# The opening of a one-core hybrid-layer kernel: reordering the transposes, the loads and the small projection that precede the steady weight stream

## The reference, cut to what matters

```python
h = rms_norm(x, lw['g_mix'])
proj = h @ lw['w_in']              # u (1024) | qkv (3072) | z (1024) | beta (8) | a (8) | two gates (2048 each)
y_s5 = s5_mixer(u, ...)            # 64 groups x 16 channels, complex diagonal state; uses s5_b, s5_c, lambda = exp(a dt)
y_dn = deltanet_mixer(qkv, z, beta, a, ...)
```

## The kernel before, in words

| slot | side jobs | units |
|---|---|---|
| 0 | const, par, x0, x1, s5a | - |
| 1 | x2, x3 | u0 |
| 2 | s5b, x4, x5 | u1 |
| 3 | s5par, h0, cst, x6, x7 | u2 |
| 4, 5, 6 | rows 0, 1, 2 | u3, u4, - |
| 7 | norm 0 | u5, u6 |
| 8, 9 | bmix 1, bmix 0 | u7 u8, u9 |
| 10 | bb 1, ct | u10, u11 |
| 11 | bb 0 | u12 |
| 12 | k0, ba | u13, u14 |
| 13 ... | s5 0 ... (three units each, then three or four) | u15 ... |

## Time and profile before

### The profile page before, as it was taken

How to read it: one execution, slowest core, us unless ns; L and a number is a source line. 1 busy time by engine, 2 the same in 40 slices (tenths; PEclk the granted TensorE clock), 3 DMA queues, 4 the chain that set the end, 5 groups by cost and what they waited for, 6 DMA issues and landing times.

```text
span 2157.6 us, 37104 instructions
## 1 busy us (share of the span) xinstructions
PE 2101.8 (97%) x14794; PEld 2050.4 (95%) x14794; DVE 1155.7 (54%) x1380; ACT 822.7 (38%) x1046; POOL 307.3 (14%) x375
## 2 busy tenths in 40 slices
PE   8989999999999999999999999999999999999997
PEld 7889999989999997999999999999999999999997
DVE  4598776945464438774444444343344444444553
ACT  6323333673232422534443333323333333333543
POOL 3634444000000104001110000000000000000111
PEclk8999999999999999999999999999999999999999
DMA  8433443543333556775444444444544444444442
GB/s 207 121 118 108 128 118 101 170 127 91 91 91 95 141 153 206 220 239 160 152 146 147 153 148 147 146 145 148 157 151 146 149 152 146 147 151 145 149 145 93
DMA packets 299266, 310.05 MB, mean 144 GB/s; under 512 B 24722, under 2 KB 290019, under 8 KB 298531
## 3 DMA queue, kind: packets, MB, share of 16 engines
q1 hardware_dynamic: 295476, 296.76, 45.0%
q0 software_dynamic: 3264, 11.64, 2.1%
q10 hardware_dynamic: 418, 0.12, 0.0%
HBM read 291.34 MB, written 17.14 MB: 143 GB/s over the span
## 4 chain that ended last, share of the span: by engine, by line
PE 88%; DVE 6%; ACT 2%; issue 2%; DMA 1%; SPq 0%; ACTq 0%; DVEq 0%
PE pg L1996 77%; PE side_a L2027 3%; DVE wlo L1329 2%; PE side_b L2027 2%; DVE cacc L1645 2%; PE side_b L2280 1%; PE side_a L2297 1%; DMA raw<-in_w_out 0%; PE side_a L1996 0%; ACT whi L897 0%; DMA par2n<-in_conv_w 0%; PE side_b L2108 0%; PE side_a L2298 0%; SPq L560 0%; PE side_a L2206 0%
## 5 line engine op out<-in xcount | busy, mean ns | idle before, releaser
L1329 DVE TENSOR_TENSOR wlo<-raw,whi 128x1024 fp32r<-128x1024 f32 (+1 forms) x528 | 647.1, 1231 | 737.7 <-ACT whi L897 736.1
L897 ACT ACTIVATE whi<-raw 128x1024 fp32r<-128x1024 f32 (+1 forms) x528 | 545.0, 1039 | 963.8 <-PE pg L1996 918.7
L1996 PE MATMUL pg<-xhi,whi 128*128 128x320 f32 x2816 | 885.0, 314 | 15.7 <-DVE wlo L1329 15.5
L1996 PE MATMUL pg<-xlo,whi 128*128 128x320 f32 x2816 | 873.8, 310 | 0.0
L1996 PE MATMUL pg<-xhi,wlo 128*128 128x320 f32 x2816 | 873.5, 310 | 0.0
L1996 PEld LDWEIGHTS pg<-xhi,whi 128*128 128x128 f32 x2816 | 532.2, 189 | 23.8 <-DVE wlo L1329 11.6
L1996 PEld LDWEIGHTS pg<-xlo,whi 128*128 128x128 f32 x2816 | 532.3, 189 | 0.8
L1996 PEld LDWEIGHTS pg<-xhi,wlo 128*128 128x128 f32 x2816 | 531.7, 189 | 0.0
L1996 PE MATMUL pg<-mhi,whi 128*128 128x320 f32 x704 | 217.7, 309 | 2.5 <-DVE wlo L1329 2.5
L1996 PE MATMUL pg<-mlo,whi 128*128 128x320 f32 x704 | 217.6, 309 | 0.0
L1996 PE MATMUL pg<-mhi,wlo 128*128 128x320 f32 x704 | 217.6, 309 | 0.0
(11 more groups left out here) (449 smaller groups left out, 2171.4 us busy)
## 6 DMA issues: line engine op xcount, KB each, us to landing
raw<-in_w_in SPq DMA_DIRECT2D x144, 512.0 KB, 3.7
raw<-in_w_gate SPq DMA_DIRECT2D x88, 512.0 KB, 3.6
raw<-in_w_up SPq DMA_DIRECT2D x88, 512.0 KB, 3.5
raw<-in_w_down SPq DMA_DIRECT2D x80, 512.0 KB, 3.6
raw<-in_w_out SPq DMA_DIRECT2D x32, 512.0 KB, 3.5
raw<-in_w_ple_gate SPq DMA_DIRECT2D x32, 512.0 KB, 3.5
raw<-in_w_a SPq DMA_DIRECT2D x16, 512.0 KB, 5.3
raw<-in_w_b SPq DMA_DIRECT2D x16, 512.0 KB, 4.5
```

The source lines that it names most:

```text
L897: act.activation(whi[:, r, 0:nk, :], raw[:, r, 0:nk, :], ACT.Copy).then_inc(w_hi, 1)
L1329: dve.tensor_tensor(wlo[:, r, 0:nk, :], raw[:, r, 0:nk, :], whi[:, r, 0:nk, :].bitcast(F32), ALU.subtract).then_inc(w_lo, 1)
L1996: ins = pe.matmul(out[:, m, 0:N], w, a, start=first and k == 0 and part == 0, stop=last and k == nk - 1 and part == 2)
```

## The change

- `side_fills` and `schedule`: x0 and x1 come ahead of par; a job `warm` holds the warm-up matmuls; `x+` is split off from x and holds ACT's `weighted` and DVE's `lows`; s5a and s5b come behind the x jobs of slots 1 and 2; s5par, h0 and cst behind x6, x7. The units of slots 10 to 14 are spread one by one.
- The store of `xt0` moves behind unit 9's load, and the four `cnat` loads move from SP's queue to POOL's, behind `tables()` and `h0_terms()`.
- `c_advanced` becomes two jobs, `cadv 0` with bb 0 and k0, and `cadv 1`; the padding becomes `pads`, the last job before s5.
- The small projection no longer uses high and low parts. DVE multiplies the 16 weight columns by the gain (`wbg`, padded to 32 columns) and PE multiplies it in plain float32 with `xt0`: 16 matmuls, feature tile k into PSUM rows 32 (k mod 4) to 32 (k mod 4) + 31. The four row groups are summed in the transposition, which multiplies by a 128 x 16 matrix `pick` of stacked identities.

```diff
-    keys = [("par",)] + [("x", j) for j in range(6)] + [("s5par",), ("h0",), ("cst",)] + [("x", j) for j in range(6, KD // 2)]
+    keys = [("x", 0), ("x", 1), ("par",)] + [("x", j) for j in range(2, KD // 2)] + [("s5par",), ("h0",), ("cst",)]
...
-    slot([("const",), ("par",), ("x", 0), ("x", 1), ("s5a",)], 0)
-    slot([("x", 2), ("x", 3)], 1)
-    slot([("s5b",), ("x", 4), ("x", 5)], 1)
-    slot([("s5par",), ("h0",), ("cst",), ("x", 6), ("x", 7)], 1)
+    slot([("const",), ("warm",), ("x", 0), ("x", 1), ("par",), ("x+", 0), ("x+", 1)], 0)
+    slot([("x", 2), ("x", 3), ("x+", 2), ("x+", 3), ("s5a",)], 1)
+    slot([("x", 4), ("x", 5), ("x+", 4), ("x+", 5), ("s5b",)], 1)
+    slot([("x", 6), ("x", 7), ("x+", 6), ("x+", 7), ("s5par",), ("h0",), ("cst",)], 1)
...
-    slot([("bb", 1), ("ct",)], 2)
-    slot([("bb", 0)], 1)
-    slot([("k0",), ("ba",)], 2)
+    slot([("bb", 1), ("ct",)], 1)
+    slot([("bb", 0), ("k0",), ("cadv", 0)], 1)
+    slot([("cadv", 1)], 1)
+    slot([("ba",)], 1)
+    slot([("pads",)], 1)
...
-                if n == 2 * RING - 1:
+                if n == 2 * RING + 1:
                     wait_drained(sp, ("x", KD // 2 - 1))
                     wait_drained(sp, ("x", KD // 2 - 2))
                     sp.dma_start(scr_x, xt0[:]).then_inc(sem("x_stored"), 16)
-                    sp.wait_ge(sem("row_squares"), 3)
-                    for r, c_ in enumerate((s5_c_re, s5_c_im)):
-                        src = c_[0].rearrange("(k g) c n -> (g c) k n", g=8)
-                        for h in range(2):
-                            sp.dma_start(cnat[:, r, :, h, :], src).then_inc(sem("cnat_landed"), 16)
...
                     elif what == "h0":
                         tables()
                         h0_terms()
+                        wait_filled(pool, ("x", KD // 2 - 2))
+                        wait_filled(pool, ("x", KD // 2 - 1))
+                        pool.wait_ge(sem("row_squares"), 3)
+                        for r, c_ in enumerate((s5_c_re, s5_c_im)):
+                            src = c_[0].rearrange("(k g) c n -> (g c) k n", g=8)
+                            for h in range(2):
+                                pool.dma_start(cnat[:, r, :, h, :], src).then_inc(sem("cnat_landed"), 16)
...
                     drain(copy(xt0[:, 2 * j:2 * j + 2, :], ps(key)[:, :, 0:N]), key)
-                    wait_drained(act, key)
-                    weighted(xt0, j, G_MIX)
+                elif what == "x+":
+                    wait_drained(act, ("x", a[0]))
+                    weighted(xt0, a[0], G_MIX)
...
                     root(a[0])
-                    act.wait_ge(sem("wba_landed"), 16)
-                    act.activation(wbhi[:], wba[:], ACT.Copy).then_inc(sem("wb_split"), 1)
...
                     b_discrete(a[0])
                     if a[0] == 0:
-                        dve.wait_ge(sem("wb_split"), 1)
-                        dve.tensor_tensor(wblo[:], wba[:], wbhi[:].bitcast(F32), ALU.subtract).then_inc(sem("wb_split"), 1)
+                        dve.wait_ge(sem("wba_landed"), 16)
+                        wait_drained(dve, ("par",))
+                        dve.wait_ge(sem("inv_ready"), 1)
+                        dve.memset(wbg[:, :, 2 * H:32], 0.0).then_inc(sem("wb_weighted"), 1)
+                        g = par1[:, G_MIX:G_MIX + KD].unsqueeze(2).broadcast_to([P, KD, 2 * H])
+                        dve.tensor_tensor(wbg[:, :, 0:2 * H], wba[:], g, ALU.mult).then_inc(sem("wb_weighted"), 1)
+                        dve.wait_ge(sem("ident_ready"), 1)
+                        dve.tensor_reduce(pick[:], ident[:].rearrange("p (q c) -> p c q", q=4)[:, 0:2 * H, :], AX.X, ALU.add).then_inc(sem("wb_weighted"), 1)
...
-                    drain(dve.tensor_copy(bafm[:], ps(key)[0:2 * H, 0, 0:N]), key)
+                    drain(dve.tensor_copy(bafm[:], ps(key)[:, 0, 0:N]), key)
...
+                elif what == "pads":
                     dve.wait_ge(sem("x_stored"), 16)
...
-                    c_advanced()
+                elif what == "cadv":
+                    c_advanced(a[0])
...
-                    pe.wait_ge(sem("wb_split"), 2)
-                    pe.wait_ge(sem("xlo_ready"), KD)
+                    pe.wait_ge(sem("wb_weighted"), 3)
+                    for j in range(KD // 2 - 2, KD // 2):
+                        wait_drained(pe, ("x", j))
                     out = begin(key)
                     for k in range(KD):
-                        for part, (w, x) in enumerate(((wbhi, xhi), (wbhi, xlo), (wblo, xhi))):
-                            ins = pe.matmul(out[0:2 * H, 0, 0:N], w[:, k, :], x[:, k, :], start=k == 0 and part == 0,
-                                            stop=k == KD - 1 and part == 2)
+                        q = k % 4
+                        ins = pe.matmul(out[32 * q:32 * q + 32, 0, 0:N], wbg[:, k, :], xt0[:, k, :], start=k < 4, stop=k >= KD - 4)
...
-                        ins = pe.transpose(out[0:n, 0, 16 * c:16 * c + 16], bafm[:, c0:c0 + n], ident[0:2 * H, 0:2 * H])
+                        ins = pe.matmul(out[0:n, 0, 16 * c:16 * c + 16], bafm[:, c0:c0 + n], pick[:], start=True, stop=True)
```

More of the change, by code:

```diff
@@ L343, in hybrid_layer @@
         wba = zpre.take("wba", [P, KD, 2 * H])
-        wbhi = zpre.take("wbhi", [P, KD, 2 * H], F32R)
         zpre2 = Zone(nc, arena_at, 8192 + 16384)
@@ L360, in hybrid_layer @@
         zba = Zone(nc, arena_at - 3 * N * 4, 3 * N * 4)
-        wblo = zba.take("wblo", [P, KD, 2 * H], F32R)
-        bafm = zba.take("bafm", [2 * H, N])
+        wbg = zba.take("wbg", [P, KD, 32])
+        bafm = zba.take("bafm", [P, N])
+        pick = zba.take("pick", [P, 2 * H])
         zd = Zone(nc, arena_at, arena)
@@ L1489, in b_discrete, with c_advanced, v @@
                     spread(bnat, 0)
-            def c_advanced():
+            def c_advanced(k):
                 wait_filled(dve, ("k0",))
[L1494 to L1508, removed]
+                tiles = slice(NT // 2 * k, NT // 2 * k + NT // 2)
+                def v(t, r):
+                    return t[:, r].rearrange("p k (q c) -> p (k q) c", q=4)[:, tiles]
+                lr, li = (sp5[:, e, tiles].unsqueeze(2).broadcast_to([P, NT // 2, 32]) for e in (3, 4))
+                tmp = ctmp[:].rearrange("p (t c) -> p t c", c=32)
+                o.step(dve.tensor_tensor(v(ctl, 0), v(ct, 0), lr, ALU.mult))
+                o.link(dve.tensor_tensor(tmp, v(ct, 1), li, ALU.mult))
+                o.step(dve.tensor_tensor(v(ctl, 0), v(ctl, 0), tmp, ALU.add))
+                o.settle()
+                o.step(dve.tensor_tensor(v(ctl, 1), v(ct, 1), lr, ALU.mult))
+                o.link(dve.tensor_tensor(tmp, v(ct, 0), li, ALU.mult))
+                dve.tensor_tensor(v(ctl, 1), v(ctl, 1), tmp, ALU.subtract).then_inc(sem("ctl_ready"), 1)
+                dve.wait_ge(sem("ctl_ready"), k + 1)
             def s5_tiles(hq):
@@ L1570, in side @@
                 what, a = key[0], key[1:]
-                if what == "x":
+                if what == "x+":
                     lows(xt0, a[0], a[0], G_MIX)
@@ L2031, in side @@
                 what, a = key[0], key[1:]
-                if what == "par":
+                if what == "warm":
                     pe.wait_ge(sem("ident_ready"), 1)
-                    out = begin(key)
+                    out = begin(("x", 0))
                     for k in range(16):
                         pe.matmul(out[:, 0, 0:P], ident[:], ident[:], start=True, stop=True)
+                elif what == "par":
                     pe.wait_ge(sem("par_landed"), 16 * 8)
+                    out = begin(key)
                     pe.transpose(out[:, 0, 0:81], par1n[:], ident[0:81, 0:81])
```

## The result

| us | before | after |
|---|---|---|
| median (6 runs each) | 2167.4 (2160.67 to 2168.64) | 2176.78 (2173.72 to 2177.89) |
| the profiled execution | 2159.32 | 2177.65 |
| its span | 2157.6 | 2175.9 |
| mean granted TensorE clock | 0.988 | 0.981 |
| first readout of s5 on PE (the **mark**) | 131.53 | 144.16 |

The ratio is 1.0048, with a 95% interval of 1.0033 to 1.0063: the change costs 9.4 us. The mark is where the opening ends and the steady stream of weights begins; most of what follows is read from it.

A forecast was written before the change was run, and what follows sets the result against it. PE, busy 97% of the span, was taken to bound the kernel. +16.0 us at u10, -5.65 and -2.1 summed to +8.2, which on the median gave 2175 us; range 2163 to 2185.

The forecast's parts named there:

- Steps 1, 2: Opening: transposes ahead of parameters gain 0.3 us at u0; later S5 scalars lose 2.4 at u2, 2.8 at u3.
- Step 3: SP's queue, free of `cnat`, loads u8 and u9 earlier: 2.4 us gained at the end of u9.
- Step 4: At `ct`, `cnat` loads behind POOL's tables make PE wait 18 us: 16 us lost at u10.
- The term for POOL's slow-down: POOL's tables and h0 terms run slower beside DVE's added splits: 1.0 us added, bounds 0 and 2.8.
- Step 5: Small projection in column groups takes 3.1 us instead of 7.12: 4 us gained.
- Step 6: `c_advanced` halved, units spread: u15's gap goes, 3.8 us of new gaps; 5.65 gained from u10 to u15, then 2.1.
- POOL doesn't gate `ct`: At `ct`, `cnat` lands before PE needs it; u10 waits only for its split: -9.7 us, 2157; chance 0.1.
- the loads drain slowly: `cnat` loads land one by one through POOL's queue; `ct` opens at 102.5: +9.5 on the forecast, 2184; chance 0.25.
- the change only shifts waits: `ct`'s wait is paid for by projection and halves: -2 to +5 us, `ct` opening at 86 to 90; chance 0.15.

The follow-up runs named there:

- e11: The kernel before with one number changed: store and `cnat` loads, still on SP's queue, two units later, behind unit 9; 2160.65 us, ratio 0.9973.
- e1: The changed kernel with the four `cnat` loads back on SP's queue, behind the store and unit 9's load; 2160.45 us, ratio 0.9974.
- e3: The changed kernel with the `cnat` loads on POOL's queue between tables and h0 terms; 2169.73 us in one run.
- e8: The kernel before with only the `cnat` loads moved behind POOL's h0 terms and the store behind unit 9; 2175.34 us, ratio 1.0053.
- e9: The kernel before with only the new order of the opening, S5 scalars later included; 2166.41 us, ratio 0.9996.
- e6: The kernel before with only the small projection changed (`wbg`, `pick`, 16 matmuls); 2159.11 us, ratio 0.9978.
- e7: The kernel before with only `c_advanced` in halves, `pads` and the units of the slots spread; 2162.91 us, ratio 0.9995.
- e10: The changed kernel with `cnat` loads on SP's queue, S5 scalars in their old places and units spread once more; 2152.50 us, ratio 0.9934.
- e2: The changed kernel with the `cnat` loads still on POOL's queue, but ahead of tables and h0 terms; 2160.44 us, ratio 0.9977.

## Why the prediction was right

The forecast was +8.2 us, 2175.0; it is +9.4, 2176.78, inside the range and in the class with the highest chance, by the mechanism foreseen. That 8.2 and 9.4 lie so near is in part luck: at the mark, where the steps can be checked, the two profiles are 12.6 us apart. Against that the steps stand like this:

| step | predicted | measured |
|---|---|---|
| 1, u0 | 20.7 | 20.74 |
| 2, wait before s5par | 3.3 | 3.18 |
| 2, u2 begins | 41.1 | 42.67 |
| 3, gap before u9; u9 | 0.6; 69.7 | 0.32; 70.59 |
| 4, tables start and end | 39.3, 84.1 | 39.49, 85.46 |
| 4, `cnat` lands; gap before `ct` | 93; 18 | 93.25; 17.16 |
| 4, u10 begins | 95.9 (+16.0) | 96.96 (+17.0) |
| 5, projection | 3.1 | 2.36 |
| 6, gaps before u12, u14 | 1.9, 1.9 | 3.10, 1.73 |
| 6, u10 to u15 | 31.8 (-5.65) | 35.1 (-2.3) |
| 6, two units from u15 | 7.1 (-2.1) | 7.1 (-2.1) |

**Steps 1, 2.** Right. u2 is 1.6 late of which 1.1 is the conv transposes: 2.75 at the lower clock, not the 1.65 of the row I used.

**Step 3.** Right in the sum (70.59 against 69.7), too small as a price. I gave SP's free queue 2.4 us; alone, without the later scalars in its way, it takes the whole gap of 3.4, and e11's interval on the whole is 2.2 to 9.8 us. The prediction had the S5 scalars eat this gain.

**Step 4.** Right in the mechanism and nearly in the size, shown from both ends (e1 to e3 take it out, e8 puts it in alone). The term for POOL's slow-down was too small: I added 1.0 us to 43.8, and the stretch took 46.0 here, 46.8 in e8 and 47.7 in e11, so 2.2 to 3.9 more. Over all profiles it took 41.8 to 48.9 us, and e9, where SP's queue is as before, has 47.0, so which part of the change slows POOL is not shown. The Trainium skill, SBUF — State Buffer, section "Who interferes with whom", has a DVE instruction with two SBUF inputs contend with a GpSimd instruction that reads SBUF; the rule goes both ways there, whichever issued first holding the other up, where the prediction named DVE alone. The 2.8 us that I worked out by that rule was nearer than my 1.0. The landing made up for it: 4.64 us behind the last issue, where I took 6 from loads of another size. `ct` took 3.7 at the lower clock, not 2.9, and u10 gave that back (3.7 for 5.3), so bb 0 began at 100.70 for 101.2.

**Step 5.** Right, 0.7 us too dear; e6 shows the gain alone.

**Step 6.** The step that failed in size: 5.65 us, of which 2.3 came. That figure held step 5's 4 us, so what it gave the halves and the spread was 1.65; measured, they cost some 2 us (2.3 less the projection's 4.3, from its first matmul to the unit behind it), though u10 was 1.6 shorter than the sum had it. Two terms did that. First, `cadv 0` took 5.4 us (104.26 to 109.65) and not 4.1: POOL's `phases(0)` ran beside it, and its operations took 0.69 to 1.12 us each where those of `cadv 1`, with POOL idle, took 0.69 throughout. Second, I let the lower clock end with u15's gap, but both new gaps brought it back, for 3.4 us each, of which PE loses half, 3.4 in all: u12 and u14 took 5.2 us each for the 3.5 that I had put down. e7 shows the outcome: alone, this part gains nothing that its interval (0.9982 to 1.0009) shows.

The **rivals**: that POOL doesn't gate `ct` falls with a gap of 17.16 that ends on the DMA. That the loads drain slowly, for 102.5, falls with the landing at 93.25. That the change only shifts waits would need `ct` open by 90.

What stays open is why the marks are 12.6 apart and the medians 9.4. The ratio's interval (7.2 to 13.7 us) holds both, the profile before is 8 us below its median and the one after 0.9 above, and marks of single executions carry the clock's stretches, 2.0 us of them in the case of e11. So the 1.2 us between forecast and median are no measure of the steps: against the marks the forecast is 4.4 short, 1.0 of it at u10 and 3.4 in step 6.

## What to carry to other kernels

A load belongs on a queue whose *preceding* work ends before the load is needed: count from the end of what is queued ahead of it, not from the queue's speed. On the fully busy engine two small gaps need not be cheaper than one larger, since each can bring the lower clock with it (both did in e7, one of e10's two did). And before four loads are moved to another engine's queue, try moving them two places down their own: here that is one changed number and worth 0.27% (0.10 to 0.45), as much as e1 with all the rest of the change.

## What the runs showed of the hardware

- The same four loads of 256 KB in 256-byte pieces take POOL 0.90 to 1.09 us each to issue, wherever they stand (after, e2), and SP's queue some 10 us in all (e1, e11). How fast they land went with what else was under way more than with who issued: 3.9 to 4.7 us in the kernel after, where SP's weights had stopped, 3.8 to 13.7 in e2, from POOL beside the stream of weights, 4.8 to 11.3 in e1, from SP.
- Sixteen float32 products of 128x32 weights and 320 columns in four column groups take 2.36 us (kernel after, e1, e6), 0.46 ns a column; the bound from k0 was 0.6. The Trainium skill, TensorEngine Tiling (Array Packing), section "Theoretical Speedup", gives up to 4 times for a dimension of at most 32; no run here has the same product in one group, so the factor isn't shown.
- The granted clock's stretches are not at the same place in executions of one opening. The window from 36 to 43 us ran at 0.52 before and at 1.00 in e11, and the edit touches nothing ahead of it. The stretch of 6.8 us is worth 3.4 of PE's time; 2.0 of them were left at u3, since e11 had begun u0 0.6 us later and waited 1.04 us for a split (42.31). Executions of the kernel before lay between 2159.45 and 2170.2, so a single profile can't show a difference of a few us; e6 and e9 were judged by nine and ten executions.
